# Merge pass of a hybrid attention/SSD layer: weight loads one unit further ahead, and a new order of splits on ScalarE

## The chip, the cores and the metric

The kernel runs on one core of a Trainium2 chip. The metric is device time in microseconds (us), the median of the runs shown. Lower is better.

## The reference

The layer takes x of 1024 rows by 1024 columns in float32. After RMSNorm one projection gives the inputs of two branches and the gate logits. Branch A is windowed attention, branch B a Mamba-2 scan with a gated norm. The part that matters here is the end:

```python
branch_a = (o_a * jax.nn.silu(z_a)) @ w_attn_proj
y_s = rms_norm(y_s * jax.nn.silu(z_s), ssd_norm_gain)
branch_b = y_s @ w_ssd_proj                      # 2048 -> 1024
gates = jax.nn.sigmoid(gate_pre + b_gate)
g_a, g_b = jnp.split(gates, 2, axis=-1)
merged = g_a * branch_a + g_b * branch_b
x = x + merged @ w_out                           # 1024 -> 1024
```

## The kernel before

All projections work in units of weights. A unit is 1024 x 128 float32 (512 KB). SyncE (SP) loads it into one of two slots of `wst` (`load_w`, L173), ScalarE (ACT) copies it rounded into the high part of `whl` (`high`, L158), and GpSimd (POOL) subtracts to give the low part (`low`, L161). TensorE (PE) then makes two groups of 24 matmuls of 512 columns, one for each half of the 1024 rows, as three products high x high, high x low, low x high (`matmuls`, L151). `whl` and `wst` have two slots each, taken in turn, so `high` of a unit waits until the unit two before it has been multiplied, and `load_w` of a unit waits until the unit two before it has been split (w_hi and w_lo). The PSUM tensor F holds two units' results, one pair of banks each.

The last block ends in three passes. Units are counted here from B3 (the first unit of the attention projection). Units 0 to 7 give branch A, 8 to 15 the first half of branch B's projection, 16 to 23 its second half. The last is the merge pass: turn n (0 to 7) merges output tile n, in which unit 16+n is the newest product. The loops run over i with s = 0, 1 inside, so n = 2i+s. Units 24 to 31 are the output projection with rows as the output (L1325). Its first group (unit 24) takes tiles 0 and 1 of the merged activations for rows 0 to 511 into M, then the same tiles for rows 512 to 1023 into F, and the latter needs all of F free: it waits for the DVE additions of turn 7 (`pair3_free`).

A turn of the merge pass, for tile n, has these steps:

- ACT: sigmoid of gate B (L1193, waits for the tile's gate and branch A, `merge_in`); `merged_high` of half 0 (L1188), `high` of unit 18+n, `merged_high` of half 1.
- POOL: gate times 1/rms (L1149, waits for the sigmoid), then `low` of unit 18+n (L161).
- DVE, for each half: sum += F (L1242, which frees the PSUM bank), sum *= gate (L1245, waits for L1149), sum += branch A's part (L1247), then after `merged_high` the low part of the merged tile (L1249, raises `m_lo`).
- SP: load of unit 18+n (18 and 19 in turns 0 and 1), wait for `m_lo` of the tile, then gate and part of tile n+2 (L1051, L1052), and x rows for the residual (L1103).

In a loop the table of ACT is loaded again ahead of the sigmoid of each even turn. Nothing else sets the order: every engine runs its instructions as written, and semaphores tie them.

Of the kernel before, what the change touches and what calls it, by code (L numbers as in the profile page):

```python
# [33 lines left out]
B2, B3, UNITS = 45, 77, 109  # L34
# [41 lines left out]
def build(nc, a, out):  # L76
# [20 lines left out]
    with root:  # L97
# [9 lines left out]
        def C(name, lo=0, hi=None):  # L107
            b, e = CONST_AT[name]
            first, tile = const_tiles[b >= BLOCK1_CONSTS]
            return tile[:, b - first + lo:(e if hi is None else b + hi) - first]  # L110
# [56 lines left out]
        def load_w(sp, u, c, at):  # L167

            if u >= 2:
                sp.wait_ge(w_hi, at * c + (u - 1))  # L170
                sp.wait_ge(w_lo, at * c + (u - 1))
            src = a["w_units"][ds(at * c + u, 1)] if c else a["w_units"][u:u + 1]
            sp.dma_start(wst[:, u % 2].rearrange("p k c -> p (k c)"), src.rearrange("a p c -> (a p) c")).then_inc(w_in[u % 2], 16)  # L173
# [859 lines left out]
        def acc_tile(i, s):  # L1033
            return acc[:, ds(i * 2 + s, 1), :].rearrange("p a t -> p (a t)")

        def row(ap):
            return ap.rearrange("a p t -> (a p) t")


        @block.sync  # L1040
        def _(sp):
            def load_gateA(i, s):
                sp.dma_start(acc_tile(i, s), row(g_d[ds(i * 2 + s, 1)])).then_inc(gateA_in[s], 16)

            def load_y(X, q0, i, s):

                sp.dma_start(tile(X, 1, i, s), row(y_d[ds(i * 2 + (q0 + s), 1)])).then_inc(y_in[s], 16)
                sp.dma_start(tile(X, 0, i, s), row(z_d[ds(i * 2 + (8 + q0 + s), 1)])).then_inc(y_in[s], 16)

            def load_merge(i, s):  # L1050
                sp.dma_start(gate[:, s, :], row(g_d[ds(i * 2 + (8 + s), 1)])).then_inc(merge_in[s], 16)  # L1051
                sp.dma_start(part[:, s, :], row(a_d[ds(i * 2 + s, 1)])).then_inc(merge_in[s], 16)  # L1052

            for s in range(2):
                sp.sem_inc(a_stored[s], 16)
            sp.wait_ge(o_stored, 16 * (NT + 1))
            sp.wait_ge(xd_ready, 4 * NT + 1)
            for k in range(NK - 1):
                sp.dma_start(X1[:, 1, k, :].bitcast(f32), o_d[k]).then_inc(o_in[k], 16)
            sp.wait_ge(yout_ready, 4 * NT + 1)  # L1060
            sp.dma_start(X1[:, 1, NK - 1, :].bitcast(f32), o_d[NK - 1]).then_inc(o_in[NK - 1], 16)
            for s in range(2):
                load_w(sp, B3 + 2 + s, 0, 0)
            for p in range(2):
                sp.wait_ge(stored[p], BLOCK1_STORES + 32 * NT)
            sp.wait_ge(y_stored, 16 * NT)
            for s in range(2):
                load_gateA(0, s)
                load_y(X0, 0, 0, s)

            with nc.sync.Fori(0, 3) as i:
                for s in range(2):
                    sp.wait_ge(gateA_ready, i * 2 + (s + 1))
                    load_gateA(i + 1, s)
                    sp.wait_ge(act_lo, i * 2 + (NK + s + 1))
                    load_y(X0, 0, i + 1, s)
                    load_w(sp, B3 + 4 + s, 2, i)

            for s in range(2):
                sp.wait_ge(unit_done, 2 * (B3 + 8))  # L1080
                sp.wait_ge(act_lo, NK + 7 + s)
                load_y(X1, 8, 0, s)

            def pass1_turn(i, s):
                load_w(sp, B3 + 10 + s, 2, i)
                sp.wait_ge(pair3_free[s], i * 2 + 2)
                sp.wait_ge(a_stored[s], i * 16 + 16)
                sp.dma_start(row(a_d[ds(i * 2 + s, 1)]), acc_tile(i, s)).then_inc(a_stored[s], 16)

            with nc.sync.Fori(0, 3) as i:  # L1090
                for s in range(2):
                    pass1_turn(i, s)
                    sp.wait_ge(act_lo, i * 2 + (NK + 9 + s))
                    load_y(X1, 8, i + 1, s)
            for s in range(2):
                pass1_turn(3, s)

            sp.wait_ge(sq_done, 16)
            for s in range(2):
                load_merge(0, s)  # L1100

            def load_rows(i, s):
                sp.dma_start(acc_tile(i, s), a["x"][ds(i * (2 * P) + s * P, P), :]).then_inc(rows_in, 16)  # L1103

            with nc.sync.Fori(0, 3) as i:
                for s in range(2):
                    load_w(sp, B3 + 18 + s, 2, i)
                    sp.wait_ge(m_lo, i * 4 + (2 * s + 2))
                    load_merge(i + 1, s)
                    load_rows(i, s)  # L1110
            for s in range(2):
                load_w(sp, B3 + 24 + s, 0, 0)
            for s in range(2):
                sp.wait_ge(m_lo, 14 + 2 * s)
                load_rows(3, s)

            with nc.sync.Fori(0, 3) as i:
                for s in range(2):
                    load_w(sp, B3 + 26 + s, 2, i)
            for c in range(2):  # L1120
                for t in range(NT):
                    sp.wait_ge(out_ready, 8 + NT * c + t + 1)
                    to = slice(c * HALF, (c + 1) * HALF)
                    sp.dma_start(out[t * P:(t + 1) * P, to], acc[:, t, to]).then_inc(out_stored, 16)
            sp.wait_ge(out_stored, 16 * 2 * NT)
# [29 lines left out]
        @block.scalar  # L1155
        def _(act):
            def silu_and_high(X, q0, i, s):

                act.wait_ge(y_in[s], i * 32 + (16 * q0 + 32))
                nc.scalar.activation(tile(X, 0, i, s), tile(X, 0, i, s), ACT.Silu).then_inc(silu3, 1)  # L1160
                act.wait_ge(gated, i * 2 + (q0 + s + 1))
                nc.scalar.activation(split_tile(X, 0, i, s), tile(X, 1, i, s), ACT.Identity,
                                     scale=C("ssd_gain", q0, q0 + 8)[:, ds(i * 2 + s, 1)]).then_inc(act_hi, 1)

            act.wait_ge(st_done, 4 * NT)
            for k in range(DVE_TILES, NK):
                act.wait_ge(o_in[k], 16)
                nc.scalar.activation(X1[:, 0, k, :], X1[:, 1, k, :].bitcast(f32), ACT.Copy).then_inc(act_hi, 1)
            with nc.scalar.Fori(0, 4) as i:
                for s in range(2):  # L1170
                    act.wait_ge(gateA_in[s], i * 16 + 16)
                    nc.scalar.activation(acc_tile(i, s), acc_tile(i, s), ACT.Sigmoid,
                                         bias=C("b_gate", 0, 8)[:, ds(i * 2 + s, 1)]).then_inc(gateA_ready, 1)
                    silu_and_high(X0, 0, i, s)
                    high(act, B3 + 2 + s, 2, i)
            with nc.scalar.Fori(0, 4) as i:
                for s in range(2):
                    silu_and_high(X1, 8, i, s)
                    high(act, B3 + 10 + s, 2, i)
                    act.wait_ge(a_stored[s], i * 16 + 32)  # L1180
                    nc.scalar.activation(acc_tile(i, s), pair3(s), ACT.Copy).then_inc(pair3_free[s], 2)
            act.wait_ge(ms_done, 1)
            nc.scalar.activation(ms, flat(M[:, 0:2, :]), ACT.Sqrt, bias=eps[:], scale=1.0 / (2 * DM)).then_inc(ms_rt, 1)

            def merged_high(i, s, h):
                act.wait_ge(acc_ready, i * 4 + (2 * s + h + 1))
                to = slice(h * HALF, (h + 1) * HALF)
                nc.scalar.activation(split_tile(X0, 0, i, s)[:, to], acc_tile(i, s)[:, to], ACT.Copy).then_inc(m_hi, 1)  # L1188

            with nc.scalar.Fori(0, 4) as i:  # L1190
                for s in range(2):
                    act.wait_ge(merge_in[s], i * 32 + 32)
                    nc.scalar.activation(gate[:, s, :], gate[:, s, :], ACT.Sigmoid,  # L1193
                                         bias=C("b_gate", 8, 16)[:, ds(i * 2 + s, 1)]).then_inc(gateB_ready, 1)
                    merged_high(i, s, 0)
                    high(act, B3 + 18 + s, 2, i)
                    merged_high(i, s, 1)
            with nc.scalar.Fori(0, 3) as i:
                for s in range(2):
                    high(act, B3 + 26 + s, 2, i)  # L1200
# [189 lines left out]
```

## Time and profile before

| | before |
|---|---|
| median of 3 runs | 1539.64 us (1538.91 to 1540.72) |
| profiled execution, first to last instruction (span) | 1529.4 us |
| median less span (launch and end around it) | 10.2 us |
| PE busy in the span | 1469.6 us (96%) |
| DVE, ACT, POOL busy | 789.6, 498.1, 475.8 us |
| merge pass on PE | 1336.8 to 1434.2 us |
| output projection on PE | 1435.3 to the end |

A separate time of the profiled execution is not recorded beside its span; the time around the span is taken from the median of the three runs. PE is nearly full in every stage, so time is to be looked for in the few places where it waits. All times in the text are microseconds from the start of the span.

### The profile page before, as it was taken

What the parts mean: (1) busy time and instruction counts of PE and PEld (TensorE: products, weight loads), DVE (VectorE), ACT (ScalarE), POOL (GpSimd) and SP (SyncE); (2) the same over time, 40 slices, a digit from 0 to 9 for tenths busy, and PEclk for the clock granted to TensorE, in tenths of its full rate; (3) what the DMA queues carried; (4) which work ended last, traced back from release to release, by engine and by line L of the source; (5) the groups of instructions that cost most, each with busy time, mean ns of one, the idle gap of its engine ahead of it and who ended that gap; (6) DMA issues with size and microseconds to landing.
All of it is one profiled execution on the core that took longest, in us unless ns stands there. A gap on an engine that the chain in (4) does not pass through costs nothing.

```text
span 1529.4 us, 22063 instructions
## 1 busy us (share of the span) xinstructions
PE 1469.6 (96%) x7744; PEld 1173.8 (77%) x7744; DVE 789.6 (52%) x977; ACT 498.1 (33%) x766; POOL 475.8 (31%) x238
## 2 busy tenths in 40 slices
PE   5999999999999998999999999999999999999999
PEld 4878888888888877777777777777777888787787
DVE  5369665444453014556565676657565554465411
ACT  6242222333322214233332424242416653332200
POOL 1122122122121232323324242332324766533321
PEclk8999999999999998999999999999999999999999
DMA  5213222222222266667666676766566636434422
GB/s 206 69 49 112 80 82 83 109 82 96 96 88 105 96 172 129 162 139 184 159 180 156 183 172 146 182 136 191 133 212 232 220 129 215 167 126 159 152 85 79
DMA packets 150328, 212.42 MB, mean 139 GB/s; under 512 B 6320, under 2 KB 111024, under 8 KB 150304
## 3 DMA queue, kind: packets, MB, share of 16 engines
q1 hardware_dynamic: 127888, 163.60, 37.8%
q10 hardware_dynamic: 20144, 39.98, 7.0%
q0 software_dynamic: 2272, 8.52, 1.4%
q8 instruction: 15, 0.25, 0.1%
q14 instruction: 9, 0.07, 0.0%
HBM read 150.87 MB, written 61.21 MB: 139 GB/s over the span
## 4 chain that ended last, share of the span: by engine, by line
PE 62%; issue 14%; DMA 10%; DVE 6%; POOL 4%; ACT 2%; SPq 1%; DVEq 0%; POOLq 0%; ACTq 0%
PE F L151 50%; DMA sb_early<-z_d 4%; DMA sb_acc<-cs_d 3%; PE F L1325 3%; PE M L1325 3%; DVE sb_early L815 2%; DMA y_d<-sb_acc 2%; POOL sb_whl L161 2%; POOL sb_res L1149 1%; SPq L633 1%; PE F L724 1%; PE F L721 1%; PE M L557 1%; POOL sb_early L970 1%; DMA g_d<-sb_res 1%
## 5 line engine op out<-in xcount | busy, mean ns | idle before, releaser
L151 PE MATMUL F<-sb_X,sb_whl 128*128 128x512 f32 x4800 | 1163.9, 402 | 7.8 <-POOL sb_whl L161 3.5
L151 PEld LDWEIGHTS F<-sb_X,sb_whl 128*128 128x128 f32 x4800 | 906.7, 190 | 245.5 <-issue 25.8
L161 POOL TENSOR_TENSOR sb_whl<-sb_wst,sb_whl 128x1024 fp32r<-128x1024 f32 x109 | 272.5, 2500 | 799.8 <-ACT sb_whl L158 799.4
L158 ACT ACTIVATE sb_whl<-sb_wst 128x1024 fp32r<-128x1024 f32 x109 | 115.1, 1056 | 259.6 <-PE F L151 117.0
L815 DVE TENSOR_SCALAR sb_early<-sb_acc,sb_ssd_sb 128x128 f32<-128x128 f32 x256 | 101.7, 472 | 11.4 <-DMA sb_acc<-cs_d 11.4
L925 ACT ACTIVATE sb_res<-F 128x512 f32<-128x512 f32 x64 | 38.2, 598 | 194.7 <-PE F L151 191.5
L477 DVE TENSOR_SCALAR sb_early<-F,sb_acc 128x1024 f32<-128x1024 f32 x24 | 30.8, 1284 | 134.7 <-PE F L151 134.7
L479 DVE SCALAR_TENSOR_TENSOR sb_early<-F,sb_acc,sb_early 128x1023 f32<-128x1023 f32 (+2 forms) x72 | 92.3, 1282 | 10.5 <-DVE sb_early L477 0.2
L794 DVE TENSOR_SCALAR M<-M,sb_cst 64x256 f32<-64x256 f32 x32 | 15.5, 483 | 156.8 <-PE M L656 156.8
L441 DVE TENSOR_TENSOR sb_early<-sb_early 32x1024 f32<-32x1024 f32 x40 | 63.3, 1581 | 30.4 <-ACT sb_early L339 29.8
L1213 DVE SCALAR_TENSOR_TENSOR sb_X<-sb_X,sb_cst x16 | 54.6, 3413 | 35.8 <-POOL sb_part L1136 35.8
L903 ACT ACTIVATE sb_early<-M,sb_early,sb_rq_sb 128x128 f32<-128x128 f32 x128 | 56.6, 463 | 15.7 <-DVE sb_early L800 15.6
L980 POOL TENSOR_TENSOR sb_acc<-sb_early,sb_cst 128x2048 f32<-128x2048 f32 x8 | 29.0, 3624 | 100.8 <-DMA y_d<-sb_acc 100.8
L918 ACT ACTIVATE sb_early<-sb_early 128x1024 f32<-128x1024 f32 x32 | 33.4, 1059 | 80.5 <-DVE sb_early L815 80.5
L663 PE MATMUL M<-sb_cst,sb_early 128*128 128x128 f32 x352 | 48.5, 279 | 9.7 <-ACT sb_early L903 9.7
L977 POOL TENSOR_TENSOR sb_part<-sb_part,sb_ssd_sb 128x512 f32<-128x512 f32 x32 | 40.3, 1266 | 54.6 <-PE F L724 54.6
L836 DVE TENSOR_TENSOR sb_early<-sb_early 128x1024 f32<-128x1024 f32 x32 | 46.9, 1485 | 14.8 <-ACT sb_early L918 13.9
L663 PEld LDWEIGHTS M<-sb_cst,sb_early 128*128 128x128 f32 x352 | 39.9, 142 | 16.4 <-ACT sb_early L903 12.2
L721 PE MATMUL F<-sb_early 128*64 128x128 f32 x512 | 35.1, 278 | 18.0 <-DVE sb_early L847 18.0
L721 PEld LDWEIGHTS F<-sb_early 128*64 128x64 f32 x512 | 27.8, 136 | 28.8 <-issue 28.8
L1210 DVE TENSOR_TENSOR sb_X<-sb_X x16 | 23.0, 1439 | 51.8 <-ACT sb_X L1160 51.8
L1325 PE MATMUL M<-sb_whl,sb_X 128*128 128x512 f32 x192 | 46.2, 396 | 1.2 <-issue 1.2
(148 smaller groups left out, 1234.4 us busy)
## 6 DMA issues: line engine op xcount, KB each, us to landing
sb_wst<-w_units SPq DMA_DIRECT2D x109, 512.0 KB, 3.5
sb_acc<-cs_d SPq DMA_DIRECT2D x8, 2048.0 KB, 22.2
x_d<-sb_res ACTq DMA_DIRECT2D x24, 512.0 KB, 2.7
z_d<-sb_res ACTq DMA_DIRECT2D x24, 512.0 KB, 2.8
sb_early<-x_d SPq DMA_DIRECT2D x8, 1024.0 KB, 8.1
sb_acc<-ecs_d SPq DMA_DIRECT2D x16, 512.0 KB, 32.2
g_d<-sb_res ACTq DMA_DIRECT2D x16, 512.0 KB, 6.6
y_d<-sb_acc POOLq DMA_DIRECT2D x8, 1024.0 KB, 15.1
```

The lines of the kernel that those rows point to most:

```text
L151: last = nc.tensor.matmul(bank, whl[:, slot, wp, k, :], act[:, ap, k, half * HALF:(half + 1) * HALF], start=(k == 0 and wp == 0 and ap == ...
L158: return nc.scalar.activation(whl[:, slot, 0], wst[:, slot], ACT.Copy)
L161: return nc.gpsimd.tensor_tensor(whl[:, slot, 1], wst[:, slot], whl[:, slot, 0].bitcast(f32), ALU.subtract)
L441: sw = nc.vector.tensor_tensor(cv[dst:dst + 32, p, :], gq[src:src + 32, p, :], sin[src:src + 32, :], ALU.mult)
L479: ins = nc.vector.scalar_tensor_tensor(acc[:, back:], raw[:, 0:T - back], tap(3 - back), acc[:, back:], ALU.mult, ALU.add)
L663: last = nc.tensor.transpose(bank[:, c * P:(c + 1) * P], src(c), C("ident"))
L721: nc.tensor.matmul(O[HD * (h % 2):HD * (h % 2) + HD, 0, (h // 2) * P:(h // 2 + 1) * P], xdt[:, g, h * HD:(h + 1) * HD], dec[:, g % 2, h, : ...
L815: last = nc.vector.tensor_scalar(dec[:, g % 2, h, :], csb[:, HG * g + h, :], cs_sb[:, ds(j, 1), HG * g + h:HG * g + h + 1].rearrange("p a ...
L836: nc.vector.tensor_tensor(dec[:, g % 2], dec[:, g % 2], cbm[:, g, :].unsqueeze(1).to_broadcast([P, HG, P]), ALU.mult).then_inc(wT_ready, 1)
L903: last = nc.scalar.activation(probs[:, r % 2, c, :], S[:, r % 2, c * P:(c + 1) * P], ACT.Exp, bias=negm[:, h:h + 1], scale=rq_sb[:, ds(j, ...
L1213: nc.vector.scalar_tensor_tensor(split_tile(X, 1, i, s), y, C("ssd_gain", q0, q0 + 8)[:, ds(i * 2 + s, 1)], tile(X, 0, i, s), ALU.mult, AL ...
L1325: last = nc.tensor.matmul(row_bank(t), X0[:, ap, k, t * P:(t + 1) * P], w_half[:, wp, (k % 2) * HALF:(k % 2 + 1) * HALF], start=(k == 0 an ...
```

## The change

SP issues the loads of units 18 and 19 ahead of its wait for the end of the second pass, and so ahead of the first gate and part loads. Each turn of its loop loads unit 20+n in place of 18+n, ahead of the same wait for `m_lo`. The two loads that stood behind the loop (24 and 25) are gone, as the loop now reaches them. ACT runs `high` of unit 18+n ahead of both `merged_high` of the tile, rather than between them.

```diff
@@ SP
             for s in range(2):
                 pass1_turn(3, s)
 
+            for s in range(2):
+                load_w(sp, B3 + 18 + s, 0, 0)
             sp.wait_ge(sq_done, 16)
             for s in range(2):
                 load_merge(0, s)
@@
             with nc.sync.Fori(0, 3) as i:
                 for s in range(2):
-                    load_w(sp, B3 + 18 + s, 2, i)
+                    load_w(sp, B3 + 20 + s, 2, i)
                     sp.wait_ge(m_lo, i * 4 + (2 * s + 2))
                     load_merge(i + 1, s)
                     load_rows(i, s)
-            for s in range(2):
-                load_w(sp, B3 + 24 + s, 0, 0)
             for s in range(2):
                 sp.wait_ge(m_lo, 14 + 2 * s)
                 load_rows(3, s)
@@ ACT
                     nc.scalar.activation(gate[:, s, :], gate[:, s, :], ACT.Sigmoid, ...
+                    high(act, B3 + 18 + s, 2, i)
                     merged_high(i, s, 0)
-                    high(act, B3 + 18 + s, 2, i)
                     merged_high(i, s, 1)
```

On ACT, in the body of the merge loop (turns with s = 0), the difference is this. L1193 is the sigmoid, L158 the weight split, L1188 the copy of a merged half tile; the lines without a tile are waits and registers.

```order
 L1193 ACT_TABLE_LOAD
 L1193 ACTIVATE sb_res<-sb_res,sb_cst 128x1024
-L1186 ISA
+L177 ISA
+L179 ISA
+L158 ACTIVATE sb_whl<-sb_wst 128x1024
+L1186 REGISTER_ALU
 L1188 ISA
 L1188 ACTIVATE sb_X<-sb_acc 128x512
-L177 ISA
-L179 REGISTER_ALU
-L158 ACTIVATE sb_whl<-sb_wst 128x1024
```

The weight split has moved to the place right behind the sigmoid, ahead of both copies of merged halves.

On SP, at the entry of the merge pass, the difference is this. L173 is a weight load, L1088 the last store of branch A's part, L1051 and L1052 the loads of gate and part.

```order
 L173 DMA sb_wst<-w_units 128x1024
 L1088 DMA a_d<-sb_acc 128x1024
+L173 DMA sb_wst<-w_units 128x1024 x2
 L1051 DMA sb_res<-g_d 128x1024
 L1052 DMA sb_part<-a_d 128x1024
 L1051 DMA sb_res<-g_d 128x1024
 L1052 DMA sb_part<-a_d 128x1024
```

Two weight loads, with their waits for the splits of units 16 and 17, now stand in the queue ahead of the first four loads of the merge.

## Rows read from the trace of the kernel before

**Rows 1.** The page's first lines: span, and busy time by engine.

```profile
span 1529.4 us, 22063 instructions
```

**Rows 2.** Timeline of PE, 1330 to 1529 (start, us, engine, line, tiles, count, idle before).

```profile
1336.80 45.36 PE L151 MATMUL F<-sb_X,sb_whl 128*128 128x512 f32 x192
1384.57 24.20 PE L151 MATMUL F<-sb_X,sb_whl 128*128 128x512 f32 x96 [2.41 <-POOL sb_whl L161]
...
1435.34 5.86 PE L1325 MATMUL M<-sb_whl,sb_X 128*128 128x512 f32 x24 [1.19 <-issue]
1441.93 5.86 PE L1325 MATMUL F<-sb_whl,sb_X 128*128 128x512 f32 x24 [0.73 <-DVEq L1243]
```

**Rows 3.** PE matmuls grouped by line, 1336.8 to 1442.

```profile
L151 PE MATMUL F<-sb_X,sb_whl 128*128 128x512 f32 x384 | 92.4, 402 | 4.9 <-POOL sb_whl L161 3.5 <-issue 1.4
```

**Rows 4.** Timeline of all engines, turn 1 and the start of turn 2.

```profile
1357.04 1.14 ACT L1193 ACTIVATE sb_res<-sb_res,sb_cst 128x1024 f32<-128x1024 f32 x1
...
1358.26 2.41 POOL L1149 TENSOR_TENSOR sb_res<-sb_res,sb_ssd_sb 128x1024 f32<-128x1024 f32 x1 [3.16 <-ACT sb_res L1193]
...
1360.70 0.69 DVE L1245 TENSOR_TENSOR sb_acc<-sb_acc,sb_res 128x512 f32 x1 [2.12 <-POOL sb_res L1149]
...
1362.27 0.63 ACT L1188 ACTIVATE sb_X<-sb_acc  x1 [4.09 <-DVE sb_acc L1247]
...
1363.66 0.68 DVE L1242 TENSOR_TENSOR sb_acc<-sb_acc,F 128x512 f32 x1
1364.50 0.69 DVE L1245 TENSOR_TENSOR sb_acc<-sb_acc,sb_res 128x512 f32 x1 [0.15 <-DVE sb_acc L1242]
...
1366.64 1.06 ACT L158 ACTIVATE sb_whl<-sb_wst 128x1024 fp32r<-128x1024 f32 x1 [3.73 <-DMA sb_wst<-w_units]
1367.60 0.61 ACT L1188 ACTIVATE sb_X<-sb_acc  x1
1367.78 2.40 POOL L161 TENSOR_TENSOR sb_whl<-sb_wst,sb_whl 128x1024 fp32r<-128x1024 f32 x1 [7.11 <-ACT sb_whl L158]
...
1368.37 2.36 DVE L1249 TENSOR_TENSOR sb_X<-sb_acc,sb_X  x1 [2.45 <-ACT sb_X L1188]
1369.53 1.15 ACT L1193 ACTIVATE sb_res<-sb_res,sb_cst 128x1024 f32<-128x1024 f32 x1
...
1373.87 0.33 SPq L173 DMA_DIRECT2D sb_wst<-w_units  x1
...
1380.84 1.06 ACT L158 ACTIVATE sb_whl<-sb_wst 128x1024 fp32r<-128x1024 f32 x1 [5.34 <-DMA sb_wst<-w_units]
```

**Rows 5.** Timeline of all engines, turn 0.

```profile
1346.91 2.42 POOL L1149 TENSOR_TENSOR sb_res<-sb_res,sb_ssd_sb 128x1024 f32<-128x1024 f32 x1 [7.71 <-DVE sb_ssd_sb L1235]
...
1353.27 2.37 DVE L1245 TENSOR_TENSOR sb_acc<-sb_acc,sb_res 128x512 f32 x1
1355.68 0.69 DVE L1247 TENSOR_TENSOR sb_acc<-sb_acc,sb_part 128x512 f32 x1
1356.51 0.63 ACT L1188 ACTIVATE sb_X<-sb_acc  x1 [3.89 <-DVE sb_acc L1247]
```

**Rows 6.** Timeline of all engines in the second pass, turn at 1242.

```profile
1244.35 2.40 POOL L1138 TENSOR_TENSOR sb_ssd_sb<-sb_ssd_sb,sb_part 128x1024 f32<-128x1024 f32 x1
1244.42 3.42 DVE L1213 SCALAR_TENSOR_TENSOR sb_X<-sb_X,sb_cst  x1 [2.23 <-POOL sb_part L1136]
```

**Rows 7.** Timeline, split of unit 17 on POOL at the entry of the pass.

```profile
1336.81 2.39 POOL L161 TENSOR_TENSOR sb_whl<-sb_wst,sb_whl 128x1024 fp32r<-128x1024 f32 x1 [3.14 <-ACT sb_whl L158]
```

**Rows 8.** DMA issues of 1358 to 1362, in their order (size, us to landing).

```profile
sb_acc<-x SPq DMA_DIRECT2D x1, 512.0 KB, 6.0
```

**Rows 9.** Timeline, turn 7: the addition that frees F.

```profile
1440.94 0.68 DVE L1242 TENSOR_TENSOR sb_acc<-sb_acc,F 128x512 f32 x1
```

**Rows 10.** Busy time in a window (PE, PEld, DVE, ACT, POOL, then PEclk, DMA, GB/s).

```profile
1385.85:1389.27 3.42, 3.42 (x10) 2.68 (x9) 1.38 (x2) 0.54 (x1) 1.28 (x1) 0.50 0.89 308
```

**Rows 11.** Timeline of PE, 1150 to 1165.

```profile
1154.90 7.03 PE L1278 MATMUL F<-sb_X,sb_whl 128*128 128x512 f32 x18 [3.74 <-DVE sb_X L1223]
```

## The prediction

> **What bounds the kernel now.** I read the page first (span 1529.4 [rows 1]; the median of the runs is 10.2 above it), then PE's timeline over the last 200 us. PE multiplies without a break for most of it; in the merge pass it waits 4.9 in three places [rows 3], then 1.19 before unit 24 and 0.73 before the second half of that unit [rows 2]. From 1441.93 on it never waits again. So whatever the change does in the merge pass reaches the end through one number: the start of that second half, now 1441.93.
>
> What does it wait for there? It needs all of F, which DVE frees with its last L1242, at 1440.94 [rows 9]; PE starts 0.99 later. Had PE never waited, eight units of 11.3 (48 matmuls at 45.36/192 = 0.236 [rows 2]) would end near 1427.5, and after 24 matmuls more the second half would start near 1433.2. The most that can be had is 8.8. Behind the 1440.94 lies the chain of turns, and that is what has to be followed, not PE's idle time.
>
> The timeline of a turn [rows 4] shows this chain. ACT's last copy of turn 0 is at 1356.51 [rows 5]; then sigmoid 1357.04, POOL's gate product 1358.26, DVE L1245 at 1360.70, first copy 1362.27, L1242 of the second half 1363.66, L1245 at 1364.50. Then ACT should copy, but its queue holds the weight split, which waits 3.73 for its weights, and it starts at 1366.64; the copy follows at 1367.60. DVE's L1249 at 1368.37 takes 2.36 instead of 0.69, since POOL's split (1367.78 to 1370.18) holds it off. Only then does SP get past its wait, and its queue issues three other loads ahead of the weights (1373.87), which reach ACT at 1380.84. That is a closed loop through SP, DMA, ACT and DVE. Each of its rounds takes about 12.4 (L1242 of the second half, 2.40 ahead of the copy at 1356.51 in turn 0, to 1440.94 in turn 7, by seven), against 11.3 on PE.
>
> **The change, part by part.** *Loads one unit ahead.* In a turn the weights for the split are now issued a whole turn earlier. Their 7 from issue to split [rows 4] lie beside the turn before, so ACT's waits on DMA go to nothing, and the loop through SP opens. If this cover were gone we would be back at the waits of now. The number of loads is the same, and a burst of SP's loads has 12 to land in.
>
> *Split first on ACT.* It starts right behind the sigmoid, if its unit two back has been multiplied. It costs ACT 0.96 (1366.64 to 1367.60) at a place where ACT otherwise waits for POOL and DVE, thus nothing on ACT. But it changes when POOL may split. ACT finishes some 2.1 after the sigmoid's start, while POOL's gate product runs from 1.22 to 3.63 after it. The weight split on POOL is therefore always ready when the gate product ends, and follows at once. DVE's L1245 waits for that same gate product. It comes at its end too, and finds POOL at work.
>
> What such a meeting costs is in the rows. L1249 met a split and ended 0.55 after it [rows 4]; L1245 of the second half in turn 0 took 2.37 [rows 5]. Who wins when both come together: in the second pass POOL started 0.07 ahead of DVE, and DVE's instruction lasted 3.42, to 1.09 after POOL's end [rows 6]. In the merge pass a second POOL instruction behind the first would start at its end or just before, DVE comes 0.03 to 0.04 after it (1358.26 + 2.41 = 1360.67, L1245 at 1360.70). So I take it that POOL wins and DVE stands for the whole 2.40, every turn.
>
> The Trainium skill, page "SBUF — State Buffer", section "SBUF: two separate sides", says the same in general: GpSimd and a VectorE operation with two SBUF inputs take a shared pair of ports as an exclusive lock, the first to start keeps it for its whole instruction and the other is fully blocked. Were it a sharing of bandwidth, L1245 would be a few tenths longer and the chain some 2 shorter per turn; the 2.37 against 0.69 [rows 5] is on the side of the lock.
>
> The new turn, from one second-half copy on ACT to the next, by the differences of starts in [rows 4, 5]: to the sigmoid 0.53; to the gate product 1.22; to its end, where the split starts, 2.37; split 2.40; blocked L1245 ends 0.54 later, L1247 starts 0.04 after that; to the first copy 0.83; to L1242 of the second half 1.39; to L1245 0.84; to L1247 0.73 (1.57 from L1245 to the copy, less 0.83); to the copy 0.83. Sum 11.72. Before an even turn the table load makes copy to sigmoid 1.93 (1367.60 to 1369.53) in place of 0.53: 13.12. Turn 0: the gate product at 1346.91 as now, split at 1349.28 to 1351.68, L1247 at 1352.26, then 0.83 + 1.39 + 0.84 + 0.73 + 0.83 = 4.62, second copy 1356.88, against 1356.51 now. Seven more turns, four odd and three even ones: 46.88 + 39.36 = 86.24, last copy 1443.12. L1242 of its second half stands 2.40 ahead of it: 1440.72, against 1440.94 now. The chain comes out **0.2 earlier**: the waits for DMA are gone, and a blocked L1245 per turn stands in their place.
>
> *SP at the entry.* The load of unit 19 waits for POOL's split of unit 17, which ends at 1336.81 + 2.39 = 1339.20 [rows 7]. The first gate and part are queued behind it. They now go first; then they will be second and third of a burst that starts near 1339.4. A third load of such a burst was issued 1.1 after the first and landed 6.0 later [rows 8], so the sigmoid of turn 0 can start near 1346.5 and the gate product near 1347.7, in place of 1346.91 (set there by the reciprocal). Bounds: 0.3, if they land as fast as a pair alone, and 1.2, if one more load's time is added. I take **0.8 later**; it goes straight into the chain.
>
> Sum of the chain: F is free 0.6 later than now, and PE's second half starts at 1442.5.
>
> *PE's clock.* Now PE's waits are small and spread. In the new order its units run close up (weights are always split in time), with about 2 of waiting for PSUM at units 22 and 23, so unit 24's first half ends near 1434 and PE then waits once, for about 8. After the wait of 2.41 at 1384.57 the granted clock was 0.50 (1.2 GHz) for a stretch, 10 matmuls in 3.42 [rows 10], and 96 matmuls took 24.20, against 22.7 by the rate before: 1.5 lost [rows 2]. After the wait of 3.74 at 1154.90 18 matmuls took 7.03 in place of 4.25: 2.8 lost [rows 11]. No wait of 8 between matmuls of this kind is in the trace. The bounds are 0 and 2.8, as the waits of 1.19 and 0.73 cost nothing and nothing shows that a longer wait costs more than one of 3.74; I take **2.1**, midway between the two rows after long waits. PE is the bound from there to the end, so it all counts. In the kernel before the 1.5 lost at 1384.57 was free, since the chain of turns was behind it.
>
> Total: -0.2 + 0.8 + 2.1 = +2.7, or 1542.3.
>
> **The rivals.** A change of 0.2% (3.1) is about what a measurement of this kernel can tell from none.
>
> *Faster: DVE gets ahead of the split.* If L1245 and L1247 slip in before POOL's split each turn, only L1249 is held off, as now. L1242 then starts 4.2 after the gate product's end instead of 5.15: 0.97 less for each of eight turns, 7.8. With -0.2 + 0.8 - 7.8 F is free at 1433.7, PE's wait is about 1.5 and cheap, and the time is 1532.4. For it: the margin is under 0.1, and the split is a new instruction at that place, with a wait of its own. Against it: [rows 6], margin 0.07, where POOL won. 0.15. Waits gone altogether (the 8.8 above, 1530.8) is the end of this same case.
>
> *Slower: the clock.* The single long wait leaves the lower clock on for longer than 5.5 of matmuls. At a half-rate matmul the loss is about 0.45 of the stretch, so the loss passes 2.5 and the sum 3.1. With the 2.8 of [rows 11] and loads that land 1.2 late the time is 1543.4. For it: a wait twice as long as any between matmuls here. Against: the case of 2.41 lost only 1.5. 0.27.
>
> *No change within 0.2%*, between these: my forecast, 0.55. The last 0.03 is for something unseen that is faster by little.
>
> **How the numbers follow.** The forecast is 1542.3, its own range 1540.3 to 1543.6 (clock loss 0.5 to 2.8, loads 0.3 to 1.2, and 0.3 for the runs' spread). The whole range reaches down a little towards the faster case, 1537.5, and up to 1544.0; it leaves out the faster case (0.15) and little else. Faster 0.18, same 0.55, slower 0.27.
>
> **What would show it.** In the new profile: L1193 and L1188 on ACT never wait for DMA; L161 starts where L1149 ends in every turn; L1245 of half 0 lasts about 2.9 in eight turns and L1249 0.69; L1149 of turn 0 starts near 1347.7; last L1242 near 1441.5; PE waits once for some 8 before the second half of unit 24, with a granted clock of 0.50 behind it. The prediction is wrong if L1245 is short (then by up to 11 on the fast side), or if the clock stays up over the long wait (then by 2).

## The result, and the profile after

The kernel after took 1547.38 us (median of 4 runs, 1544.77 to 1549.89), the kernel before 1539.76 (median of 4, one run more than in the table above); the ratio is 1.0044, 95% interval 1.003 to 1.0058. It is slower, by some 4.6 to 8.9 us, where 1542.3 and "most likely no change" had been forecast, with 0.27 for slower. In a second job, below, the same kernel came out at 1.0036 (1.0024 to 1.0048).

The first view is PE's timeline of the kernel after over the same stretch as [rows 2]:

```profile
1344.64 1.88 PE L1301 MATMUL M<-sb_ssd_sb,sb_cst 128*128 128x512 f32 x4
1345.95 45.36 PE L151 MATMUL F<-sb_X,sb_whl 128*128 128x512 f32 x192
...
1417.04 11.46 PE L151 MATMUL F<-sb_X,sb_whl 128*128 128x512 f32 x48 [1.74 <-DVEq L1243]
...
1440.13 5.76 PE L1325 MATMUL M<-sb_whl,sb_X 128*128 128x512 f32 x24
1453.79 7.71 PE L1325 MATMUL F<-sb_whl,sb_X 128*128 128x512 f32 x24 [7.89 <-DVEq L1243]
```

Two things are to be seen. The waits for POOL's split are gone. What is left is four short waits for DVE behind the 192nd matmul (3.2 together, the longest is shown) and one of 7.89 for DVE ahead of unit 24's second half, with the group behind it slowed (7.71 for 24 matmuls, 5.86 before). And the pass begins at 1345.95, 9.15 later than in [rows 2], though nothing ahead of it was changed. So absolute starts can't be compared; I count from the pass's first matmul. The second half of unit 24 starts at 107.84 counted so (before 1441.93 - 1336.80 = 105.13), and from its start to the end of the span it takes 89.3 (before 87.5). Pass and tail together are 4.6 longer.

The timeline of all engines of the kernel after, turns 0 and 1, answers to [rows 4, 5]:

```profile
1348.82 0.42 SPq L1051 DMA_DIRECT2D sb_res<-g_d  x1
1349.29 0.42 SPq L1052 DMA_DIRECT2D sb_part<-a_d  x1
...
1356.08 1.28 ACT L1193 ACT_TABLE_LOAD   x1 [6.85 <-DMA sb_part<-a_d]
1357.38 1.15 ACT L1193 ACTIVATE sb_res<-sb_res,sb_cst 128x1024 f32<-128x1024 f32 x1
1358.43 1.04 ACT L158 ACTIVATE sb_whl<-sb_wst 128x1024 fp32r<-128x1024 f32 x1
1358.60 2.41 POOL L1149 TENSOR_TENSOR sb_res<-sb_res,sb_ssd_sb 128x1024 f32<-128x1024 f32 x1 [10.25 <-ACT sb_res L1193]
1360.97 2.39 POOL L161 TENSOR_TENSOR sb_whl<-sb_wst,sb_whl 128x1024 fp32r<-128x1024 f32 x1
1361.05 2.86 DVE L1245 TENSOR_TENSOR sb_acc<-sb_acc,sb_res 128x512 f32 x1 [4.68 <-POOL sb_res L1149]
...
1364.88 0.63 ACT L1188 ACTIVATE sb_X<-sb_acc  x1 [5.40 <-DVE sb_acc L1247]
...
1370.43 2.42 POOL L1149 TENSOR_TENSOR sb_res<-sb_res,sb_ssd_sb 128x1024 f32<-128x1024 f32 x1 [7.08 <-ACT sb_res L1193]
...
1372.81 2.40 POOL L161 TENSOR_TENSOR sb_whl<-sb_wst,sb_whl 128x1024 fp32r<-128x1024 f32 x1
1372.89 2.87 DVE L1245 TENSOR_TENSOR sb_acc<-sb_acc,sb_res 128x512 f32 x1 [2.14 <-POOL sb_res L1149]
```

POOL's split (L161) starts where the gate product ends, 0.08 ahead of DVE's L1245, and L1245 takes 2.87 (2.81 to 2.88 in the eight turns) in place of 0.69. That is the blocked product of the forecast, and it is there in all eight turns: the gate products start at 12.65, 24.48, 37.64, 49.47, 62.61, 74.44, 87.58 and 99.39 from the pass's start, turns of 11.8 and 13.1. What was not forecast is the first of these numbers. In the kernel before it was 10.11 (1346.91). The part of the first tile lands 6.8 after its issue at 1349.29, and only behind that wait does ACT load its table (1.28), then the sigmoid. In the kernel before the gate data was there already when the table was loaded, and both stood beside DVE's reciprocal, for which the gate product waited anyway:

```profile
1340.10 1.28 ACT L1193 ACT_TABLE_LOAD   x1
1340.11 6.55 DVE L1235 RECIPROCAL sb_ssd_sb<-sb_ssd_sb 128x1024 f32<-128x1024 f32 x1 [5.35 <-ACT sb_ssd_sb L1183]
1341.39 1.15 ACT L1193 ACTIVATE sb_res<-sb_res,sb_cst 128x1024 f32<-128x1024 f32 x1
```

One thing more is in these rows. The semaphore for which the sigmoid waits (`merge_in`) counts the gate's load and the part's, though the sigmoid reads only the gate. The gate, issued at 1348.82, landed 5.1 later, near 1353.9, some 2.1 ahead of the end of the wait. By these rows a wait for the gate alone would have let the gate product start about 2.1 earlier. This is an estimate, and no run here tests it.

The last view is the clock, in a window from where it falls to where it is up again (columns as in [rows 10]):

```profile
1451.06:1457.89 6.83, 4.11 (x10) 3.24 (x11) 3.57 (x6) 1.26 (x2) 0.00 (x0) 0.50 0.05 5
```

The granted clock is 0.50, the 1.2 GHz level, for the last 2.7 of the long wait and for the ten matmuls behind it.

### The profile page after: what moved, and what is told of

It reads as the page before. It is cut to its first block, busy times and chain, and to the rows that moved or that the text cites. A ratio compares the mean times of both kernels' runs of the same rounds, so it can differ in the third digit from the quotient of the medians.

```text
span 1543.1 us, 22063 instructions
## 1 busy us (share of the span) xinstructions
PE 1471.6 (95%) x7744; PEld 1174.8 (76%) x7744; DVE 809.0 (52%) x977; ACT 498.0 (32%) x766; POOL 477.4 (31%) x238
## 3 DMA queue, kind: packets, MB, share of 16 engines
q0 software_dynamic: 2272, 8.52, 1.4%
## 4 chain that ended last, share of the span: by engine, by line
PE 63%; DMA 16%; issue 10%; DVE 5%; POOL 3%; ACT 2%; SPq 1%; DVEq 0%; ACTq 0%; POOLq 0%
PE F L151 51%; DMA sb_early<-z_d 8%; DMA sb_acc<-cs_d 5%; PE F L1325 3%; DMA g_d<-sb_res 3%; PE M L1325 3%; POOL sb_whl L161 2%; PE F L724 2%; PE F L721 1%; DVE sb_early L815 1%; PE M L734 1%; SPq L633 1%; PE M L557 1%; POOL sb_res L1149 1%; DMA sb_acc<-consts 1%
## 5 line engine op out<-in xcount | busy, mean ns | idle before, releaser
L161 POOL TENSOR_TENSOR sb_whl<-sb_wst,sb_whl 128x1024 fp32r<-128x1024 f32 x109 | 272.9, 2504 | 749.4 <-ACT sb_whl L158 748.9
L158 ACT ACTIVATE sb_whl<-sb_wst 128x1024 fp32r<-128x1024 f32 x109 | 115.0, 1056 | 249.5 <-PE F L151 125.9
L815 DVE TENSOR_SCALAR sb_early<-sb_acc,sb_ssd_sb 128x128 f32<-128x128 f32 x256 | 112.0, 511 | 25.9 <-DMA sb_acc<-cs_d 25.8
L721 PE MATMUL F<-sb_early 128*64 128x128 f32 x512 | 37.7, 292 | 25.1 <-DVE sb_early L847 24.9
L836 DVE TENSOR_TENSOR sb_early<-sb_early 128x1024 f32<-128x1024 f32 x32 | 51.9, 1640 | 14.1 <-ACT sb_early L918 13.1
L721 PEld LDWEIGHTS F<-sb_early 128*64 128x64 f32 x512 | 29.8, 145 | 35.9 <-issue 35.1
L1325 PE MATMUL F<-sb_whl,sb_X 128*128 128x512 f32 x192 | 48.0, 407 | 7.9 <-DVEq L1243 7.9
L1325 PEld LDWEIGHTS F<-sb_whl,sb_X 128*128 128x128 f32 x192 | 37.4, 195 | 17.4 <-issue 8.3
```

What stands on the lines that cost most here:

```text
L158: return nc.scalar.activation(whl[:, slot, 0], wst[:, slot], ACT.Copy)
L161: return nc.gpsimd.tensor_tensor(whl[:, slot, 1], wst[:, slot], whl[:, slot, 0].bitcast(f32), ALU.subtract)
L721: nc.tensor.matmul(O[HD * (h % 2):HD * (h % 2) + HD, 0, (h // 2) * P:(h // 2 + 1) * P], xdt[:, g, h * HD:(h + 1) * HD], dec[:, g % 2, h, : ...
L815: last = nc.vector.tensor_scalar(dec[:, g % 2, h, :], csb[:, HG * g + h, :], cs_sb[:, ds(j, 1), HG * g + h:HG * g + h + 1].rearrange("p a ...
L836: nc.vector.tensor_tensor(dec[:, g % 2], dec[:, g % 2], cbm[:, g, :].unsqueeze(1).to_broadcast([P, HG, P]), ALU.mult).then_inc(wT_ready, 1)
L1325: last = nc.tensor.matmul(row_bank(t), X0[:, ap, k, t * P:(t + 1) * P], w_half[:, wp, (k % 2) * HALF:(k % 2 + 1) * HALF], start=(k == 0 an ...
```

## The experiments

Each kernel was timed together with the kernel before on the same chip. The table holds what each profile gave; "half" is the start of unit 24's second half from the pass's first matmul, "tail" from there to the end of the span, both in us. The rows of each that carry the argument follow.

| kernel | first gate product | half | tail | ratio to before (95%) |
|---|---|---|---|---|
| before | 10.11 | 105.13 | 87.5 | |
| control (before again) | 10.11 | 104.01 | 87.5 | 1.0009 (0.999 to 1.0027) |
| after | 12.65 | 107.84 | 89.3 | 1.0044 (1.003 to 1.0058) |
| after again | 12.59 | 107.82 | 89.7 | 1.0036 (1.0024 to 1.0048) |
| loads only | 12.44 | 101.98 | 87.4 | 1.0008 (0.9989 to 1.0027) |
| split first only | 10.11 | 129.18 | 89.9 | 1.0176 (1.0153 to 1.0199) |
| after, gate loads first | 10.12 | 105.16 | 90.3 | 1.0027 (1.001 to 1.0043) |
| after, PE kept busy | 12.38 | 107.57 | 87.4 | 1.0022 (1.001 to 1.0033) |
| after, split before gate | 15.40 | 109.30 | 88.9 | 1.0043 (1.0027 to 1.006) |
| loads ahead, gate loads first | 10.11 | 99.73 | 90.1 | 0.9979 (0.9968 to 0.999) |
| the same, ACT's loop written out | 10.11 | 95.60 | 87.4 | 0.9952 (0.9939 to 0.9964) |

**Control.** The kernel before with no edit.

> The kernel before once more, for its spread and for a second profile. The profile of the kernel before reached the merge pass 9.1 earlier than that of the kernel after, though nothing ahead of the pass is changed. If that is chance of the execution (my theory), the stages ahead of the pass take some other time again here, by several us, while from the pass's first matmul to the second half of unit 24 it is again 105.1 +/- 0.5. If the change did something to the stages ahead of the pass (rival), this profile reaches the pass within 1 of 1336.8. Ratio 1.000.

PE's timeline of the control:

```profile
1346.04 45.36 PE L151 MATMUL F<-sb_X,sb_whl 128*128 128x512 f32 x192
1392.69 11.44 PE L151 MATMUL F<-sb_X,sb_whl 128*128 128x512 f32 x48 [1.29 <-POOL sb_whl L161]
...
1450.05 5.87 PE L1325 MATMUL F<-sb_whl,sb_X 128*128 128x512 f32 x24 [0.75 <-DVEq L1243]
```

The pass is reached at 1346.04, as with the kernel after. So the 9.15 ahead of the pass are no effect of the change; the first profile of the kernel before was an uncommonly fast execution. Where it was faster can be read: in the scan of branch B (L721 on PE), between 607 and 1156. The first two rows are the kernel before, the last two the control.

```profile
L721 PEld LDWEIGHTS F<-sb_early x512: 132/137/137, 607.9 to 1141.8; 128*64 128x64 f32 x171
L815 DVE TENSOR_SCALAR sb_early<-sb_acc,sb_ssd_sb 128x128 f32<-128x128 f32 x240 | 98.5, 485 | 11.4 <-DMA sb_acc<-cs_d 11.4
L721 PEld LDWEIGHTS F<-sb_early x512: 132/137/231, 607.5 to 1151.1; 128*64 128x64 f32 x171
L815 DVE TENSOR_SCALAR sb_early<-sb_acc,sb_ssd_sb 128x128 f32<-128x128 f32 x240 | 120.4, 576 | 25.6 <-DMA sb_acc<-cs_d 25.6
```

The eleven profiles begin L721 between 606.4 and 608.2 and end it between 1141.8 and 1156.0; from there to the pass each takes 194.8 to 195.6. Within 600 to 1160 DVE waited 11.4 for the loads of `cs_d` in the first profile and 17.6 to 26.9 in the others, and its L815 took longer. Why it varies is not shown. Half came out at 104.01, 1.1 below the first profile and outside the half microsecond expected: the loop of the kernel before contains the landing of weights. ACT's waits for them sum to 25.1 in the pass of the first profile and to 23.9 here, which is the difference:

```profile
ACT sb_whl L158 <- DMA sb_wst<-w_units: 25.1, 6, 5.3
ACT sb_whl L158 <- DMA sb_wst<-w_units: 23.9, 6, 4.2
```

In this job 29 runs of the kernel before spread from 1534.9 to 1547.9, where the three known at first had spread by 1.8.

**Loads only.**

```diff
@@ ACT, from the kernel after
-                    high(act, B3 + 18 + s, 2, i)
                     merged_high(i, s, 0)
+                    high(act, B3 + 18 + s, 2, i)
                     merged_high(i, s, 1)
```

> Only the loads are moved ahead; ACT copies, splits, copies as before. Theory of the port (the split on POOL right behind the gate product blocks DVE for 2.4 in each turn; between the copies it blocks 1.7): turns of 11.3 and 12.7 in place of 11.7 and 13.1, second half of unit 24 at 102 from the pass's start (before 105.1, after 107.8), so 1.5 to 4 faster than after by the chain, and about 1 to 3 faster than before with the lower clock after the long wait counted. Rival, that the loads ahead of the gate loads cost all of it and the order on ACT nothing: the same as after, 107.8, ratio 1.004.

Half is at 101.98 (102 expected), 5.9 below the kernel after. The timeline of one turn shows what the split between the copies does:

```profile
1388.43 0.69 DVE L1245 TENSOR_TENSOR sb_acc<-sb_acc,sb_res 128x512 f32 x1 [3.54 <-POOL sb_res L1149]
...
1391.49 0.68 DVE L1242 TENSOR_TENSOR sb_acc<-sb_acc,F 128x512 f32 x1
1391.74 2.40 POOL L161 TENSOR_TENSOR sb_whl<-sb_wst,sb_whl 128x1024 fp32r<-128x1024 f32 x1 [3.35 <-ACT sb_whl L158]
1392.32 2.37 DVE L1245 TENSOR_TENSOR sb_acc<-sb_acc,sb_res 128x512 f32 x1 [0.15 <-DVE sb_acc L1242]
```

L1245 of the first half is free (0.69); POOL's split now starts 0.58 ahead of L1245 of the second half, so that part of it lies beside work that it doesn't hold up. It costs 1.7 (2.37 against 0.69), where L1245 of the kernel after costs 2.2 (2.87). Two turns take 24.0 in place of 25.0. The last 2.0 of the 5.9 come in turn 7: there F is freed before the held L1245, and from the last gate product to half it takes 6.41, where the kernel after takes 8.45. In the turn shown L1242, which reads F in PSUM, takes 0.68 from 1391.49, though the split starts at 1391.74: it is not held.

By pass and tail this kernel is 2.1 to 3.2 faster than the two profiles of the kernel before. The timed ratio does not show it: 1 to 3 us faster was expected, and 1.0008 with its interval can't be told from no change, nor from 1.7 faster.

**Split first only.** The other part of the change alone.

```diff
@@ ACT, from the kernel before
+                    high(act, B3 + 18 + s, 2, i)
                     merged_high(i, s, 0)
-                    high(act, B3 + 18 + s, 2, i)
                     merged_high(i, s, 1)
```

> Only the order on ACT is changed; the weights are loaded as before. If the loop of now runs through SP and the weights' landing, both copies now stand behind the weights: 7.0 from issue to split, 7.9 from split to the last low part, 3.1 through SP's queue, 18 per turn in place of 12.4, and about 30 us slower than before (ratio 1.018 to 1.024). Rival, that the loads ahead hide nothing that matters: turns stay below 13 and the time is within 5 us of before.

Ratio 1.0176, some 27 us slower. From its timeline:

```profile
1408.00 0.33 SPq L173 DMA_DIRECT2D sb_wst<-w_units  x1
...
1414.75 1.06 ACT L158 ACTIVATE sb_whl<-sb_wst 128x1024 fp32r<-128x1024 f32 x1 [8.44 <-DMA sb_wst<-w_units]
1415.71 0.61 ACT L1188 ACTIVATE sb_X<-sb_acc  x1
```

ACT waits 8.44 for weights ahead of both copies. Behind a first turn of 11.6, whose weights were there in time, they take 18 and 15 in alternation, by the starts of the gate products (18 expected for all; why every second one is shorter was not followed up), and the ratio is just below the range expected. So the loop through SP and the landing is real. Half is 24.0 later here than in the next kernel, which has the same order on ACT, the same first gate product and the loads one unit ahead: these loads are what makes the new place of the split bearable, and the two parts of the change are not independent.

**After, gate loads first.**

```diff
@@ SP, from the kernel after
-            for s in range(2):
-                load_w(sp, B3 + 18 + s, 0, 0)
             sp.wait_ge(sq_done, 16)
             for s in range(2):
                 load_merge(0, s)
+            for s in range(2):
+                load_w(sp, B3 + 18 + s, 0, 0)
```

> The kernel after, with the first four loads of gate and part ahead of the loads of units 18 and 19, as before. If the late gate loads cost what the profile of after shows (gate product of turn 0 at 12.65 from the pass's start in place of 10.1), the second half of unit 24 starts at 105.3 in place of 107.8 and the time is 2.5 below after: 1.5 to 2.5 slower than before, by the clock alone (ratio 1.001 to 1.0025). Rival, that the late start is made up for by later turns: no difference from after (1.0044).

The first gate product waits for the reciprocal again, at 10.12, and half is at 105.16 (105.3 expected). The timeline at the entry:

```profile
1349.68 1.28 ACT L1193 ACT_TABLE_LOAD   x1
1356.49 2.39 POOL L1149 TENSOR_TENSOR sb_res<-sb_res,sb_ssd_sb 128x1024 f32<-128x1024 f32 x1 [7.71 <-DVE sb_ssd_sb L1235]
1358.92 0.69 DVE L1245 TENSOR_TENSOR sb_acc<-sb_acc,sb_res 128x512 f32 x1 [2.13 <-POOL sb_res L1149]
```

The order of the first loads thus costs 2.7 of the 107.84: 2.5 by the late gate product, carried through eight turns, and 0.2 in turn 0, where the weights now come later and L1245 is free. What is left of the change, loads ahead and split first, leaves the chain where it was (105.13) or 1.1 longer (104.01). The ratio of 1.0027 is a little above the range expected, and its interval meets that of the kernel after; it is the profiles that tell the two apart. The tail was 90.3 here, 2.8 more than with the clock up, after the same kind of wait:

```profile
1451.53 8.67 PE L1325 MATMUL F<-sb_whl,sb_X 128*128 128x512 f32 x24 [7.90 <-DVEq L1243]
```

**After again.** No edit.

> The kernel after once more, for its spread over many runs and a second profile. The merge pass should repeat: second half of unit 24 at 107.8 +/- 0.3 from the pass's start, and from there 89 to 90.5 to the end (87.4 where the clock stays up). With the kernel before at 104.0 to 105.1 and 87.45 that makes 4.5 to 7 slower, ratio 1.003 to 1.0045. Where the profile reaches the pass is chance: 1336 to 1352.

Half 107.82, tail 89.7, ratio 1.0036: the chain of the kernel after repeats within 0.02 here, and within 0.3 in the next run (107.57), where that of the kernel before, with its waits for weights, moved by 1.1.

**After, PE kept busy.** 29 matmuls without use are added in the long wait.

```diff
@@ PE, from the kernel after
-            with nc.tensor.Fori(0, 2) as c:
+            for c in range(2):
...
                         if k == 0 and t0 == 4:
+                            if c == 0:
+                                pe.wait_ge(pair3_free[0], 24)
+                                for n in range(29):
+                                    nc.tensor.matmul(F[:, 0, :], X0[:, 0, 0, 0:P], w_half[:, 0, 0:HALF],
+                                                     start=True, stop=True)
                             for p in range(2):
                                 pe.wait_ge(pair3_free[p], 24)
```

> The kernel after, with the loop over the two column halves of the output projection written out, and 29 matmuls of 512 columns (6.8 us) into a free bank of F, whose result is not used, in the one long wait of PE. If the clock that falls behind the long wait costs 1.5 to 2.8 after it, the granted clock now stays at 1.00 and from the second half of unit 24 to the end it takes 87.4 in place of 89.3 to 90.3: 2 to 3 below after, unit 24's second half still at 107.8 from the pass's start. Rival, that the lower clock is no cost of the wait (a slower first group for another reason): still 89 or more.

In PE's timeline the added matmuls are L1322, and unit 24 is L1330:

```profile
1442.33 6.93 PE L1322 MATMUL F<-sb_whl,sb_X 128*128 128x512 f32 x29
1450.38 5.83 PE L1330 MATMUL F<-sb_whl,sb_X 128*128 128x512 f32 x24 [1.11 <-issue]
```

The group behind the wait takes 5.83 again, the tail is 87.4, and the granted clock stays at 1.00 over the gap and the group:

```profile
1442.30:1450.30 8.00, 6.96 (x30) 5.26 (x28) 4.84 (x4) 1.15 (x2) 4.42 (x2) 1.00 0.20 66
1450.38:1456.05 5.67, 5.67 (x25) 4.58 (x26) 2.07 (x3) 0.63 (x1) 0.00 (x0) 1.00 0.29 82
```

With PE at work in the gap the clock does not fall; in all four profiles in which it stood still there for 7.9 to 8.2 the clock fell. Work thrown away in the gap wins the loss back: 2.3 by the tail of the kernel after in the same job (89.7 against 87.4), 0.0014 of ratio, with intervals that overlap. The loop over the column halves was written out too; what that does by itself was not run.

**After, split before gate.** With the gate loads first, and in a turn on ACT `high`, then the sigmoid; on POOL `low`, then the gate product.

```diff
@@ ACT and POOL, from the kernel with the gate loads first
+                    high(act, B3 + 18 + s, 2, i)
                     act.wait_ge(merge_in[s], i * 32 + 32)
                     nc.scalar.activation(gate[:, s, :], gate[:, s, :], ACT.Sigmoid,
                                          bias=C("b_gate", 8, 16)[:, ds(i * 2 + s, 1)]).then_inc(gateB_ready, 1)
-                    high(act, B3 + 18 + s, 2, i)
...
+                    low(pool, B3 + 18 + s, 2, i)
                     pool.wait_ge(gateB_ready, i * 2 + (s + 1))
                     nc.gpsimd.tensor_tensor(gate[:, s, :], gate[:, s, :], ms, ALU.mult).then_inc(gr_ready, 1)
-                    low(pool, B3 + 18 + s, 2, i)
```

> As gate_loads_first, but in each turn ACT splits ahead of the sigmoid and POOL splits ahead of its gate product, so that POOL is idle when DVE starts its three additions and products. Theory of the port and the chain: L1245 and L1249 last 0.69 in all turns; but the split itself still stands in the chain (copy to split 0.53, to POOL 1.14, split 2.35, gate product 2.44, then 5.37 to the next copy: 11.8), now in even turns too, as the table load hides beside POOL's split. Turn 0 starts late, the gate product waits for unit 16 and the split, at 15.0 from the pass's start, then 7 turns of 11.8: second half of unit 24 at 104.3 (gate_loads_first 105.2), and ratio 1.0015 to 1.0025. Rival, that L1245 is slow for another reason than POOL's split: it stays at 2.9 and the turns grow to 13 and more, second half at 113.

Half is at 109.30, 5 more than expected. Its timeline says why, and what held:

```profile
1381.07 0.63 ACT L1188 ACTIVATE sb_X<-sb_acc  x1 [3.15 <-DVE sb_acc L1247]
1381.72 1.28 ACT L158 ACT_TABLE_LOAD   x1
...
1384.09 1.28 ACT L1194 ACT_TABLE_LOAD   x1
...
1384.15 2.40 POOL L161 TENSOR_TENSOR sb_whl<-sb_wst,sb_whl 128x1024 fp32r<-128x1024 f32 x1 [8.46 <-ACT sb_whl L158]
...
1389.06 0.69 DVE L1245 TENSOR_TENSOR sb_acc<-sb_acc,sb_res 128x512 f32 x1 [5.92 <-POOL sb_res L1150]
```

All sixteen L1245 last 0.69: with POOL idle there, DVE is never held. The rival (L1245 slow for another reason) is out. From an even turn to the odd one behind it takes 11.9 (11.8 expected). But from an odd one to the next even one it takes 13.3: the loop's body now begins with a copy, and a table load of 1.28 was put ahead of that too, on the chain. My count had it beside POOL's split. The ratio, 1.0043, is above the range expected, as the later half would have it.

**Loads ahead, gate loads first.** ACT as before, SP as in the kernel after but for the entry.

```diff
@@ from the kernel with the gate loads first
-                    high(act, B3 + 18 + s, 2, i)
                     merged_high(i, s, 0)
+                    high(act, B3 + 18 + s, 2, i)
                     merged_high(i, s, 1)
```

> Loads one unit ahead, ACT in the order of the kernel before, and the first gate and part ahead of the weights of units 18 and 19. The two gains add: gate product of turn 0 at 10.1 (loads only: 12.4), second half of unit 24 at 99.6 (loads only 102.0, kernel before 104.0 to 105.1). PE's wait there is near 1.5 and the clock stays up: 4 to 5.5 faster than before, ratio 0.9965 to 0.9975. If the port does not matter (rival) it is the same as with the split first and the gate first (105.2).

Half 99.73 (99.6 expected); the two gains add. The ratio, 0.9979, is short of the expected one, for this reason:

```profile
1443.90 8.52 PE L1325 MATMUL F<-sb_whl,sb_X 128*128 128x512 f32 x24 [3.48 <-DVEq L1243]
```

The wait is 3.48, not 1.5 (PE's units closed up), and the clock fell about it here: 8.52 for the group, tail 90.1. With loads only, a wait of 3.51 left the clock up (5.85 for the group, tail 87.4). After waits of the same length it went one way in one profile and the other way in the other.

**The same, ACT's loop written out.**

```diff
@@ ACT, from loads ahead, gate loads first
-            with nc.scalar.Fori(0, 4) as i:
+            for i in range(4):
                 for s in range(2):
                     act.wait_ge(merge_in[s], i * 32 + 32)
```

> As loads_gate_first, with ACT's merge loop written out, so that its table is loaded once and not once in two turns. If the table load lies on the chain of turns, as I counted it, each of three turns is 1.35 to 1.4 shorter, the chain would end at 95.6 and PE becomes the bound of the pass: second half of unit 24 at 96 to 97.5, 7 to 8 faster than before, ratio 0.995. Rival, that the table load hides under the wait for POOL or DVE: 99.6 as without it.

Its timeline of PE, and its row of table loads in the pass (grouped by line):

```profile
1344.10 90.16 PE L151 MATMUL F<-sb_X,sb_whl 128*128 128x512 f32 x384
1434.10 5.76 PE L1325 MATMUL M<-sb_whl,sb_X 128*128 128x512 f32 x24
1439.70 5.53 PE L1325 MATMUL F<-sb_whl,sb_X 128*128 128x512 f32 x23
```

```profile
L1193 ACT ACT_TABLE_LOAD x1 | 1.3, 1283 | 0.0
```

One table load of this line in place of four, all turns 11.0 to 11.2, and PE never waits: 384 matmuls in 90.16, half at 95.60, a little below the 96 expected. F is free 2.65 before PE comes to it, so PE bounds the pass. By the profiles 4.1 of the gain over the kernel just before come from the chain and 2.7 from the clock, which stays up as PE does not wait. This kernel is 0.48% faster than the one before (1528.74 against 1536.23 in its job), the best of the study.

## Why the prediction was right or wrong

**What bounds the kernel: right.** The start of unit 24's second half decides, and the chain of turns behind it. Where the chain runs faster than PE nothing is left to win in the pass (the last kernel).

**Loads one unit ahead hide 7 per turn: right.** No ACT instruction waits for weights in the pass of the kernel after, and without the loads the new order costs some 27. But the first sigmoid does wait for a DMA (6.85), where the signs named in the prediction had ACT never waiting for one.

**POOL wins the port, DVE stands for the whole split: right.** 0.08 of a margin, L1245 at 2.87, turns of 11.8 and 13.1 (11.72 and 13.12 forecast; the missing 0.1 is L1247 starting 0.13 behind L1245 in place of 0.04). The lock of the Trainium skill, page "SBUF — State Buffer", section "SBUF: two separate sides", is what this trace shows. From the first gate product to the last L1242 it took 94.2, 93.8 forecast.

**The first gate loads: the step that failed.** "I take 0.8 later" (bounds 0.3 and 1.2) is the term of the sum that was mis-sized: it measured 2.5, and moving these loads alone takes 2.7 back. I compared the landing with the reciprocal of 1346.91 and put the sigmoid right at the landing. But the table load stands between: behind the wait, not ahead of it, and 1.28 long. The sum counts such a load ahead of each even turn and leaves it out of turn 0. In the kernel before it was hidden there, as the data had landed by then. The landing itself was 0.4 later than taken. So the chain was 2.7 longer than in the first profile of the kernel before, and not 0.6.

**The clock: right in kind and size.** 2.1 forecast; 1.8, 2.2 and 2.8 measured behind waits of 7.9, 1.5 behind one of 8.2, and nothing of it with PE kept busy. That the size came so near is in part luck: the same wait gives anything between 1.5 and 2.8.

**The base and the range.** With 2.5 in place of 0.8 the sum is +4.4, and the two profiles differ by 4.6 in pass and tail. The timed ratio says 6.8 with an interval of 4.6 to 8.9. Against the control, whose chain was 1.1 shorter, the difference is 5.7 by the same count (197.2 against 191.5). The rest, some 1 to 2, is within what the scan scatters: profiles reached the pass between 1336.8 and 1351.6, all with the same code up to there. The bounds of the terms, with 0.3 at either end, would give 1539.9 to 1543.7, not 1540.3 to 1543.6; the result is outside of either. My range took 0.3 for the runs' spread from three runs that happened to lie close; and I read "the median is 10.2 above the span" as launch, while in every later run time and span differ by under 2. With 1.7 around it, the first profile was of an execution of about 1531.1, some 8.5 faster than the median; this is an estimate, as its own time is not recorded. Why the scan scatters stays open; no run here was aimed at it.

**The rivals.** "DVE gets ahead" did not happen. "Slower" came true, by another mechanism than the one named for it: the clock's loss was about as forecast and would not have passed the 0.2% alone; the late start of turn 0 came on top of it.

## What to carry to other kernels

When a wait is moved or lengthened, look for what the engine does between the wait and the instruction that counts: a table load behind a semaphore added its 1.28 to the wait here, and it came again in each pass of ACT's loop (four loads; one with the loop written out). A split of weights on GpSimd of 2.40 cost VectorE 2.2 where it started 0.08 ahead of a product with both inputs in SBUF, 1.7 where it started 0.58 ahead, and nothing of an addition that reads PSUM, so put it where VectorE reads PSUM or waits for someone else. And two loads that are ahead of need must not stand in the queue in front of one that is needed at once: here that cost 2.7.

## What the runs showed of the hardware that was not expected

- Executions of the same kernel spread by 13 us (1534.9 to 1547.9 in 29 runs of one job), and the medians of the kernel before in three jobs were 1540.9, 1536.2 and 1541.9. In the profiles the spread ahead of the pass lies in the scan, which takes 533.9 to 548.8 from its first to its last weight load on PE. Only ratios within a job, and stretches counted from a common instruction, can be compared.
- After waits of PE of 3.48 and 3.51 before the same group of matmuls the clock fell in one profile (tail 90.1) and stayed up in the other (87.4).
- A loop on ScalarE whose body begins with a copy and goes on to a sigmoid got a table load ahead of both (1381.72 and 1384.09). The body that begins with the sigmoid got one in each pass of the loop, ahead of the sigmoid, and as straight code one in all.
